# DeltaNet heads: inverse and transpose under separate semaphores, a head's gated output and residual moved, the first head's conversion, queue and gate reordered

## The reference

```
q, k, v = silu(causal_conv4(h @ w_in)) per head;  z = h @ w_z;  q, k l2-normalised
beta = sigmoid(..);  g = cumsum of the log decay in each chunk of 64
lower  = strict_tril((k*beta) @ k.T * decay)          per chunk
sol    = solve(I + lower, [v*beta, k*beta*exp(g)])    unit lower triangular
for each chunk:
    v_new = u - w @ state
    o     = (q*exp(g)) @ state + tril(q @ k.T * decay) @ v_new
    state = state*exp(g_last) + k_dec.T @ v_new
out = (rmsnorm(o) * silu(z)) @ w_out
```

## Time and profile before

| | us |
|---|---|
| median of three runs | 1420.49 (1419.34 to 1420.56) |
| the profiled execution | 1417.11 |
| its span, first to last instruction | 1415.4 |
| mean granted TensorE clock in it | 0.993 |

### The profile page before, as it was taken

The page is one execution under the profiler, slowest core; times in us unless marked ns, Lnnn a source line. Parts: engine busy times, 40 slices in busy tenths (PEclk is TensorE's granted clock), DMA queues, the critical chain, the costliest instruction groups (busy, mean ns, idle before and its releaser), DMA issues.

```text
span 1415.4 us, 18106 instructions
## 1 busy us (share of the span) xinstructions
PE 1360.9 (96%) x6594; PEld 1120.3 (79%) x6594; DVE 791.6 (56%) x1205; ACT 533.4 (38%) x901; POOL 252.4 (18%) x243
## 2 busy tenths in 40 slices
PE   7899999999899999999999999989999999999998
PEld 5678878888778888888888878758888888888877
DVE  5557777777674343343456677674443434435655
ACT  6444445444154132231334431453332313223344
POOL 3654545453030000000002110002010000000211
PEclk9899999999999999999999999999999999999999
DMA  6233233222323223223322352503322232223221
GB/s 176 65 84 78 60 81 84 55 61 69 99 77 117 90 91 117 89 89 102 105 89 82 97 100 66 115 6 108 116 90 89 89 119 89 89 89 104 85 80 60
DMA packets 168575, 125.67 MB, mean 89 GB/s; under 512 B 35873, under 2 KB 165186, under 8 KB 168514
## 3 DMA queue, kind: packets, MB, share of 16 engines
q1 hardware_dynamic: 167410, 123.01, 29.2%
q10 hardware_dynamic: 1104, 1.84, 0.5%
HBM read 116.96 MB, written 5.25 MB: 86 GB/s over the span
## 4 chain that ended last, share of the span: by engine, by line
PE 75%; DVE 11%; ACT 3%; issue 3%; DMA 3%; DVEq 2%; POOL 2%; POOLq 0%; SPq 0%; ACTq 0%
PE psum L148 22%; PE psum L150 21%; PE psum L149 21%; DMA xScaled<-inv_blocks 2%; PE psum L890 2%; DVE wL L140 1%; PE psum L900 1%; ACT wH L132 1%; DMA inv_blocks<-blk 1%; DVE bL L1397 1%; DVE hT L1598 1%; DVEq L1168 1%; DVE terms L1166 1%; DVE acc L1596 1%; PE psum L1917 1%
## 5 line engine op out<-in xcount | busy, mean ns | idle before, releaser
L148 PE MATMUL psum<-aH,wH 128*128 128x512 f32 x896 | 361.2, 403 | 8.3 <-issue 5.4
L150 PE MATMUL psum<-aL,wH 128*128 128x512 f32 x896 | 351.3, 392 | 0.0
L149 PE MATMUL psum<-aH,wL 128*128 128x512 f32 x896 | 350.5, 391 | 0.0
L140 DVE TENSOR_TENSOR wL<-wRaw,wH 128x2048 fp32r<-128x2048 f32 (+2 forms) x125 | 241.0, 1933 | 128.5 <-ACT wH L132 122.9
L148 PE MATMUL psum<-bH,wH 128*128 128x512 f32 x720 | 284.8, 396 | 2.3 <-DVE pleT L2043 1.6
L150 PE MATMUL psum<-bL,wH 128*128 128x512 f32 x720 | 280.9, 390 | 0.0
L149 PE MATMUL psum<-bH,wL 128*128 128x512 f32 x720 | 280.8, 390 | 0.0
L132 ACT CAST wH<-wRaw 128x2048 fp32r<-128x2048 f32 (+2 forms) x109 | 196.9, 1813 | 219.9 <-PE psum L150 219.9
L148 PEld LDWEIGHTS psum<-aH,wH 128*128 128x128 f32 x896 | 169.4, 189 | 42.0 <-issue 6.8
L150 PEld LDWEIGHTS psum<-aL,wH 128*128 128x128 f32 x896 | 169.0, 189 | 36.2
L149 PEld LDWEIGHTS psum<-aH,wL 128*128 128x128 f32 x896 | 169.6, 189 | 32.1 <-issue 0.5
(11 more groups left out here) (295 smaller groups left out, 1498.6 us busy)
## 6 DMA issues: line engine op xcount, KB each, us to landing
wRaw<-in_mlp_w_up SPq DMA_DIRECT2D x64, 512.0 KB
wRaw<-in_mlp_w_down SPq DMA_DIRECT2D x64, 512.0 KB
wRaw<-in_dn_w_in SPq DMA_DIRECT2D x32, 512.0 KB
wRaw<-in_ple_w_gate SPq DMA_DIRECT2D x16, 512.0 KB
xScaled<-inv_blocks SPq DMA_DIRECT2D x16, 256.0 KB, 3.2
wRaw<-in_sw_w_in SPq DMA_DIRECT2D x16, 256.0 KB
wRaw<-in_sw_w_out SPq DMA_DIRECT2D x16, 256.0 KB
wRaw<-in_dn_w_out SPq DMA_DIRECT2D x8, 384.0 KB
```

The costliest lines, as they stand in the source:

```text
L140: last = [nc.vector.tensor_tensor(o, r, h_.bitcast(F32), ALU.subtract) for o, r, h_ in zip(*([v if half is None else v[:, half * v.shape[1 ...
L148: nc.tensor.matmul(o, wh, xh, start=first, stop=False)
L149: nc.tensor.matmul(o, wl, xh, start=False, stop=False)
L150: return nc.tensor.matmul(o, wh, xl, start=False, stop=last)
```

## The change

Five things are done.

1. `blk_out` and `blk_in` become two semaphores each, one for the inverse and one for the transpose. SP waits for the inverse's store and issues its load, then waits for the transpose's store and issues its load. `lower(0)` waits for the inverse alone, `corner(0)` for the transpose too.
2. `blocks_sp` is cut in two: `lower_sp` has the store and load of `low`. In the loop it stands at the end of the body for the next head. Before the loop it stands ahead of the load of panel 4.
3. At the end of a step DVE does `tail(2)` before `masked(2)`, and ACT does `tail(1)` before `inverse(1)`.
4. The conversion of panel 2 goes ahead: on ACT behind the taps of head 0's k, on DVE behind the silu of head 0's q. The taps of head 0's v go ahead of `decC` on POOL. In the first step PE does `fill(2)` before it waits for `ss_ok`.
5. In the first step DVE does the silu of head 1's q before `blocks_inverse(8)`, instead of after `attT`.

```diff
-        blk_out = sem("blk_out")
-        blk_in = sem("blk_in")
+        blk_out = [sem(f"blk_out{w}") for w in range(2)]
+        blk_in = [sem(f"blk_in{w}") for w in range(2)]
...
-        def blocks_sp(sp, a):
+        def lower_sp(sp, a):
             lo = lowD.ap().unsqueeze(0)
             sp.wait_ge(low_ok, a + 1)
             sp.dma_start(whole(lo)[:, 0], lowT).then_inc(low_out, 16)
             sp.wait_ge(low_out, 16 * a + 16)
             sp.dma_start(lowBlk[0:NB, 0:B16 * B16].rearrange("b (r c) -> b r c", c=B16), diagonal(lo)[:, 0]).then_inc(low_in, 16)
+
+        def blocks_sp(sp, a):
+
             sp.wait_ge(blk_ok, a + 1)
             for w in range(2):
-                sp.dma_start(diagonal(invD.ap())[:, w], blk[0:NB, w, 0:B16 * B16].rearrange("b (r c) -> b r c", c=B16)).then_inc(blk_out, 16)
-            sp.wait_ge(blk_out, 32 * a + 32)
+                sp.dma_start(diagonal(invD.ap())[:, w], blk[0:NB, w, 0:B16 * B16].rearrange("b (r c) -> b r c", c=B16)).then_inc(blk_out[w], 16)
             for w, dst in enumerate((inv, invT)):
-                sp.dma_start(dst, whole(invD.ap())[:, w]).then_inc(blk_in, 16)
+                sp.wait_ge(blk_out[w], 16 * a + 16)
+                sp.dma_start(dst, whole(invD.ap())[:, w]).then_inc(blk_in[w], 16)
...
-            for n in range(2, 5):
+            for n in range(2, 4):
                 load_panel(sp, n // 2, n % 2)
             sp.wait_ge(blank_out, 32)
+            lower_sp(sp, 0)
+            load_panel(sp, 2, 0)
             with sp.Fori(0, HEADS_A - 3) as a:
                 blocks_sp(sp, a)
                 load_panel(sp, a + 2, 1)
                 load_panel(sp, a + 3, 0)
+                lower_sp(sp, a + 1)
...
             def lower(i):
                 if i == 0:
-                    pe.wait_ge(blk_in, 32 * a + 32)
+                    pe.wait_ge(blk_in[0], 16 * a + 16)
...
@@ corner(i), i == 0 @@
                     pe.wait_ge(att_ok, a + 1)
+                    pe.wait_ge(blk_in[1], 16 * a + 16)
...
@@ dn_step_pe @@
             if b is None:
                 gram_kk()
-            pe.wait_ge(ss_ok, 2 * a + 2)
-            solve(0)
-            if b is not None:
+                fill(2)
+                pe.wait_ge(ss_ok, 2 * a + 2)
+            else:
+                pe.wait_ge(ss_ok, 2 * a + 2)
+                solve(0)
                 gram_kk()
-            update(0)
-            fill(2)
+                update(0)
+                fill(2)
...
@@ dn_step_act @@
             z_act(act, a)
-            if b is None:
-                prep_hi(act, n - 1, 0)
             prep_hi(act, n, 1)
...
+            tail(1)
             inverse(1)
-            tail(1)
...
@@ dn_step_dve @@
             stt(out=work[:, 6, :], in0=bank[BZ], scalar=-1.0, in1=work[:, 7, :], op0=ALU.mult, op1=ALU.mult).then_inc(low_ok, 1)
-            if b is None:
-                prep_lo(dve, n - 1, 0)
             advance(0)
...
             solved(2)
+            if b is None:
+                silu_dve(dve, p, 0, s, reused)
             blocks_inverse(8)
...
-            if p is not None:
+            if p is not None and b is not None:
                 silu_dve(dve, p, 0, s, reused)
...
+            tail(2)
             masked(2)
-            tail(2)
             tail(3)
             grown(2)
...
@@ dn_step_pool @@
-            if b is None:
-                taps_pool(pool, a, 2)
...
@@ dn_act @@
-            for b in range(2):
-                taps_act(act, 0, b, first=True)
-                tanh_act(act, 0, b)
+            taps_act(act, 0, 0, first=True)
+            tanh_act(act, 0, 0)
+            taps_act(act, 0, 1, first=True)
+            prep_hi(act, 2, 0)
+            tanh_act(act, 0, 1)
...
@@ dn_dve @@
-            for b in range(2):
-                silu_dve(dve, 0, b, 0, False)
+            silu_dve(dve, 0, 0, 0, False)
+            prep_lo(dve, 2, 0)
+            silu_dve(dve, 0, 1, 0, False)
...
@@ dn_pool @@
             taps_pool(pool, 0, 1)
+            taps_pool(pool, 0, 2)
             dn_step_pool(pool, None, 0, 1, 1)
```

More of the change, by code:

```diff
@@ L656, in dn_sp @@
             dn_out_load(sp, 0)
+            lower_sp(sp, HEADS_A - 2)
             blocks_sp(sp, HEADS_A - 2)
@@ L659, in dn_sp @@
             dn_out_load(sp, 2)
+            lower_sp(sp, HEADS_A - 1)
             blocks_sp(sp, HEADS_A - 1)
```

## The result

On one chip, run in turns with the kernel before, the changed kernel took 1403.06 us (median of 4) against 1419.91 (median of 4): a ratio of 0.989 with an interval of 0.987 to 0.992. One of the four, at 1694.13, was disturbed and is not in the ratio; the median of the other three is 1401.97. The profiled execution took 1400.85 us, its span 1399.1. The forecast was 1407.2 with a range of 1403 to 1415: faster, as predicted, and 4 to 5 us further than predicted. The stated range is met at its very edge (1403.06) or missed by 1 us (1401.97), and the forecast's own range, 1404 to 1410, is missed either way. Against the profiled execution of before, from which the sum was made, it is 1417.11 - 1400.85 = 16.3 us where 13.3 were predicted.

The account below looks back on a forecast made before the run. TensorE, holding matmuls for 96% of the span, was taken as the bound. 8.5 + 2.5 - 0.3 + 3.2 = 13.9, less 0.6 for the clock, gives 13.3 us off the median 1420.49: 1407.2 us, range 1403 to 1415.

Parts of the forecast that it names:

- Part 1: Return of the inverted blocks: with its own semaphore the inverse's load is issued 0.45 us earlier; 8.5 us won over seven heads.
- Rival (b): Stores and loads share engines, so the inverse lands as late as the transpose; 4.8 us left, 1415.7 us; chance 0.09.
- Part 2: End of a head's step: gated output and residual moved, TensorE's waits at the next step's start go; 2.5 us less 0.3.
- Part 3: First head's reordering: the triangular inverse's first product starts at 83.4 instead of 86.56 us; 3.2 us won.
- four chances in ten of one: First head's two new TensorE pauses: chance of one spell at the lower clock, deducted as 0.6 us.
- two spells of 1.5: First head before the change, 61.90 to 86.50 us: two spells at 1.2 GHz, costing 3.0 us, counted as gone.
- rival (a): First head gives nothing: parked DVE and a lower clock eat its 3.2 us; 1410.4 to 1412.8 us; chance 0.18.
- (e): First head: TensorE's clock falls after both new pauses; 10.9 us left, 1409.6 us; chance 0.12.
- Rival (c): Heads' step: another chain just behind, DVE's to the block copy, binds; only 0 to 2 us, 1419 us; chance 0.05.
- Rival (d): Head's end: ACT's transpose copy, behind y's rounding, stalls TensorE in seven heads; at 2.5 us each 1424 us; chance 0.06.

## Why the prediction was right, and where its sizes were off

**Part 1, the semaphores: right, 8.5 us predicted, 9.4 to 9.8 measured.** The mechanism is in the rows: the first load goes out 0.54 us sooner behind the store (0.45 forecast), L898 waits in no head from 1 to 6 and 1.3 us in the last (1.2 forecast). Rival (b), that the inverse lands only with the transpose, is out. What I sized wrongly is the worth of a wait: I took the view's waits, 8.8, and even a little less, and each of the six also held the 0.16 us of normal overlap. The "few tenths" that I deducted did not stay.

**Part 2, the moved tail: right in place, too small in size, 2.2 predicted, 3.4 to 4.0 measured.** This is the term that was mis-sized. The same reading of waits from the shown end was at fault, and more so, since the waits are short and many: six at L840, two at L853. 4.5 us went between `decay` and update, 0.2 to 0.8 came back between `lower` and `decay` (0.3 deducted).

**Part 3, the first head: the size came out, by a path that was only partly mine.** Forecast 3.2 at `lower`, measured 3.8 and 4.2 there and 3.7 and 4.1 at the first `decay`. `lower`'s store at 62.09 (62.5 forecast), DVE parked for 1.7 us before the silu instead of 4, the block copied at 77.8 (78.6), two pauses of 1.8 and 1.2 (and 1.2 earlier, at L778, behind POOL's late addition, in one of the two profiles) instead of 2.2 and 2.9. The pause before L898 was short because the five units ahead of it ran at the lower clock: from 76.23 to 81.53, 5.30 us. Where they didn't, in the change without the tail, they took 3.71 and the pause is 2.60. The windows of the changed kernel against the earlier trace rows (columns as there):

```profile
62.09:86.50 24.41, 21.38 (x95) 17.14 (x94) 14.03 (x27) 8.53 (x12) 11.31 (x10) 0.93 0.48 121
75.90:79.40 3.50, 3.17 (x9) 2.48 (x10) 2.35 (x4) 2.06 (x2) 3.00 (x3) 0.62 0.12 13
```

That is one spell at the lower level, where the text gave four chances in ten of one, and in the stretch of the earlier trace rows the clock is 0.93 for 0.88. It cost nothing: it covered time in which TensorE would have waited for the block anyway, and `lower` starts at 82.49 and 82.62 in the two kernels without it and at 82.33 to 82.74 in the three with it. That was luck of place, not forecast. The text also misread the kernel before: the 3.0 us that it gives to two spells of 1.5 are one spell, from about 61 to 67 us (granted 0.50 from 62 to 66), so its price of 1.5 a spell came from no spell there. The spells of the change's first head are shorter; one behind `lower` costs 1.6 us. What the prediction missed is that this part is not independent of part 1. Alone it gave nothing that can be timed, as rival (a) had it, and in its trace for a reason in the manner of (e): the pause before `lower` was longer and slow products came behind it. That such a pause brings them each time is refuted above, so how much of the difference belongs to part 1 stays open. I had added the parts as if they were independent.

**The rest.** Rival (c), another chain just behind, is out: everything won in the heads reached the end, within the 4 us by which the stretch behind them moves from run to run. Rival (d) did not happen and is real: 7.3 us when it was made to. A head's step is (345.12 - 118.89)/6 = 37.7 us, where 38.4 was forecast and (362.69 - 123.94)/6 = 39.8 was before; the forecast started from 40.0. The gain is 2.1 us a step where 1.6 was forecast, 2.9 us over six steps, nearly all of the 3.0 by which the sum came out too small.

## What to carry to other kernels

Where two transfers are waited for together and the first consumer needs one of them, give each its own semaphore and chain its load to its own store: here that was 9 to 10 of 16 us. Price a stall on TensorE by the distance between starts, in the stalled flow and in a flow without a stall: a wait shown as 0.3 us was worth 0.46 to 0.57 here. And before adding up edits in one place, ask whether one changes a pause that another leaves: head 0 won 1.1 us in the trace with the reordering alone, lost 1.6 with the semaphores alone, and won 3.7 and 4.1 with all of it.

## What the runs showed of the hardware

A pause of 2.3 to 2.7 us before head 0's `lower` was followed by slow products in four of six profiles, and cost 1.6 us between `lower` and `decay` there. A pause of 2.4 to 2.6 before the last head's `lower` was followed by them in one of four (the change with one semaphore: the eight products took 2.08 us instead of 1.16). The pause of 1.8 before the five units ahead was followed by a slow spell in five of seven. The length of the pause alone does not decide it, and no run here tells what does. Such a spell costs nothing where TensorE would have stood anyway.

Small DVE operations met POOL's additions. Copies of one shape, 32x256, took 0.36 us with POOL idle, 0.53 where one POOL operation ended beside them, and 1.24 where another had begun 0.03 us before; two 32x64 operations took 0.42 alone and 2.3 beside an addition. So a reordering on DVE that looks free can move an instruction into POOL's way.
